# A fused attention stage: the next head's queries turned in pieces, and part of a mix moved to GpSimd

## The chip, the cores and the metric

The kernel runs on one core of one Trainium2 chip. The time is device microseconds of one execution of the whole program, here as a median over runs. The engines are named as in the profile: PE (TensorE), DVE (VectorE), ACT (ScalarE), POOL (GpSimd) and SP (SyncE).

## The reference, cut to what matters

The reference is a transformer of two blocks on 1024 rows of width 1024. The change touches only the differential attention of its first layer. That has four heads; each has two maps of 64 channels, 1024 queries, and 1280 keys (256 of the context and 1024 of the sequence), with values of 128 channels:

```python
s = jnp.einsum('bqhmd,bkhmd->bhmqk', qblk, k) * ATTN_SCALE   # m = 0, 1
p = jax.nn.softmax(s, axis=-1)
a = p[:, :, 0] - lam * p[:, :, 1]
return jnp.einsum('bhqk,bkhv->bqhv', a.astype(v.dtype), v)
```

Everything is float32. Before it stand the projections and a Fourier transform, behind it an output product, a convolution layer and a feed-forward layer; none of these is changed.

## The kernel before

**Tiles.** A head is worked in eight tiles (t = 0 to 7) of 128 queries, four heads one after the other. One loop over h = 0 to 2 ends with the passage to head h + 1 and its first two tiles; the last head is written out behind the loop. For a tile:

- PE makes the scores of map 0 and map 1, six matmuls each (`scores`, L1195), into one three-bank region of PSUM for each map.
- DVE takes the negative maximum over 1280 columns of each map (`peaks`, L1497).
- ACT exponentiates each map and sums the rows (`exps`, L859).
- DVE takes reciprocals (L1505), makes the weight of map 1 (L1507), and mixes the two maps, `mixed = prob1 * weight + prob0`, first columns 0 to 511 (`combine`), then 512 to 1279 (`combine_rest`); both are L1517.
- PE turns the mixed tile in three rounds of 4, 4 and 2 blocks (`turn`, L1211), all through the one PSUM bank MIX_BANK; DVE copies the first round out (L1532), ACT the other two (L867).
- PE multiplies by the values (`values`, L1223), and ACT finishes the tile (L876, L879).

**Order.** Each engine has its own stream, and the order in it is written out by hand; semaphores join them. In the stream of PE, `tile_step` has for tile t the scores of map 0, the second round of tile t - 2, the scores of map 1, the third round and the values of tile t - 2, and the first round of tile t - 1. In that of DVE it has for tile t the peaks of map 0, `combine` of tile t - 1, the peaks of map 1, `combine_rest` of tile t - 1, and the copy of the first round of tile t - 1.

**Passage to the next head.** Keys and queries of the next head must be turned and split into a high and a low part. POOL copies them in doubled form into `k_head` and `q_head` (L971) long ahead. At the passage PE turns the keys into the two score regions (`turn_k`, L470, ten blocks a map), ACT writes the high part (L488), DVE the low part (L497); then the same for the queries in two pieces of 1024 columns, also through the score regions (`turn_q` L470, `high_q` L493, `low_q` L504). So the first scores of the next head wait for all of it.

**POOL** has besides these copies only, in the last head, two splits of weight tiles of the next product (`out_lo`, L132, 128x1024).

## Time and profile before

| what | value |
|---|---|
| median of 3 runs | 1808.62 us (1808.35 to 1814.71) |
| span of the profiled execution, first to last instruction | 1803.4 us |
| PE, PEld busy in the span | 1742.9 us (97%), 1461.8 us (81%) |
| DVE, ACT, POOL busy | 1212.7 us (67%), 800.6 us (44%), 759.5 us (42%) |
| mean granted TensorE clock | 0.991 |

No device time is given for the profiled execution beside its span; the median of the runs stands 5.2 us above the span. The attention stage lies between about 360 and 595 us of the span. In timeline rows the first column is the start in us, the second the time until the end, then engine, line, operation, output and inputs, and in brackets the engine's idle time ahead of it and what ended it. Operations of an engine overlap a little, so the distance between two starts is shorter than the first one's duration.

### The profile page before, as it was taken

Reading aid. Unit: us, or ns where it says so; the run is one execution under the profiler, and the core shown is the slowest. Engines: PE = TensorE matmul, PEld = TensorE weight load, DVE = VectorE, ACT = ScalarE, POOL = GpSimd, SP = SyncE. Lnnn points to the kernel's source line nnn. Section 1 sums busy time; section 2 is a strip of 40 time slices with the busy share of each in tenths; the row PEclk is TensorE's granted clock in tenths of the full one; section 3 lists DMA queues with packets and bytes.
Section 4 is the critical chain, followed back from the end, with each engine's and each line's share of the span. In section 5 each row is a group of like instructions: output and inputs, shape, how many; then the busy total and the mean of one; then the engine's idle time right before and its main releaser. Section 6 shows DMA issues by size and latency. Waiting matters only on the chain.

```text
span 1803.4 us, 22828 instructions
## 1 busy us (share of the span) xinstructions
PE 1742.9 (97%) x8677; PEld 1461.8 (81%) x8677; DVE 1212.7 (67%) x1390; ACT 800.6 (44%) x1253; POOL 759.5 (42%) x450
## 2 busy tenths in 40 slices
PE   6999999989998899999999999999999999999999
PEld 4788887888888688788888889978888888878887
DVE  3734799578898616854545743786666667689865
ACT  3522222667677325533333432754435444444443
POOL 2332422000001142466666520548999999810000
PEclk8999999999999999999999999999999999999999
DMA  9567123000000731222221611303232232286433
GB/s 358 204 216 238 48 83 117 4 24 1 0 0 1 245 106 47 59 82 59 60 81 59 198 59 47 117 24 106 82 93 83 72 92 82 85 329 223 147 122 123
DMA packets 165385, 188.32 MB, mean 104 GB/s; under 512 B 9454, under 2 KB 117543, under 8 KB 165159
## 3 DMA queue, kind: packets, MB, share of 16 engines
q1 hardware_dynamic: 165287, 187.00, 31.7%
q8 instruction: 64, 1.05, 0.2%
q14 instruction: 34, 0.28, 0.1%
HBM read 152.37 MB, written 34.60 MB: 104 GB/s over the span
## 4 chain that ended last, share of the span: by engine, by line
PE 53%; DVE 4%; ACT 2%; issue 1%; DMA 1%; SPq 0%; ACTq 0%; DVEq 0%
PE ps L3217 20%; PE ps L2225 15%; PE ps L3268 10%; PE ps L2285 5%; PE ps L3568 1%; PE ps L3230 1%; DVE cv_lo_p L132 1%; DVE up_lo_p L132 1%; DVE residual L2147 0%; ACT residual L3404 0%; PE ps L3234 0%; DVE residual L3126 0%; DMA w_raw<-in_ffn_w_out 0%; ACT cv_hi_p L129 0%; ACT residual L1964 0%
## 5 line engine op out<-in xcount | busy, mean ns | idle before, releaser
L3217 PE MATMUL ps<-up_hi_p,st_hi_p 128*128 128x512 f32 x560 | 218.7, 391 | 2.9 <-ACT residual L2935 2.9
L3217 PE MATMUL ps<-up_lo_p,st_hi_p 128*128 128x512 f32 x560 | 218.5, 390 | 0.0
L3217 PE MATMUL ps<-up_hi_p,st_lo_p 128*128 128x512 f32 x560 | 218.3, 390 | 0.0
L3268 PE MATMUL ps<-down_ring 128*128 128x512 f32 x924 | 210.9, 390 | 2.8 <-DVE down_ring L132 2.6
L3268 PEld LDWEIGHTS ps<-down_ring 128*128 128x128 f32 x924 | 173.0, 188 | 40.5 <-issue 4.0
L132 POOL TENSOR_TENSOR in_lo<-in_raw,in_hi 128x512 fp32r<-128x512 f32 (+1 forms) x54 | 96.9, 1803 | 215.5 <-ACT in_hi L129 215.5
L2225 PE MATMUL ps<-cv_hi_p,cv_st_hi_p 128*128 128x512 f32 x392 | 153.2, 391 | 2.7 <-ACT residual L1943 2.7
L2225 PE MATMUL ps<-cv_hi_p,cv_st_lo_p 128*128 128x512 f32 x392 | 153.0, 390 | 0.0
L2225 PE MATMUL ps<-cv_lo_p,cv_st_hi_p 128*128 128x512 f32 x392 | 153.0, 390 | 0.0
L2067 DVE TENSOR_TENSOR residual<-ps,residual 128x512 f32<-128x512 f32 x70 | 48.3, 691 | 120.0 <-PE ps L2225 120.0
L132 POOL TENSOR_TENSOR st_lo_p<-up_raw,st_hi_p 128x512 fp32r<-128x512 f32 x68 | 101.7, 1499 | 64.4 <-ACT st_hi_p L129 64.4
L3217 PEld LDWEIGHTS ps<-up_hi_p,st_hi_p 128*128 128x128 f32 x560 | 105.5, 188 | 25.4 <-issue 3.3
L3217 PEld LDWEIGHTS ps<-up_lo_p,st_hi_p 128*128 128x128 f32 x560 | 105.6, 189 | 21.9
L3217 PEld LDWEIGHTS ps<-up_hi_p,st_lo_p 128*128 128x128 f32 x560 | 105.6, 189 | 21.9
L3068 DVE TENSOR_TENSOR residual<-ps,residual 128x512 f32<-128x512 f32 x100 | 68.4, 686 | 69.5 <-PE ps L3217 69.2
L1497 DVE TENSOR_REDUCE neg_peak<-ps 128x1 f32<-128x1280 f32 x64 | 95.2, 1487 | 9.8 <-PE ps L1195 8.6
L983 PE MATMUL ps<-in_hi,h_hi 128*128 128x512 f32 x256 | 99.8, 390 | 1.6 <-issue 0.9
L983 PE MATMUL ps<-in_hi,h_lo 128*128 128x512 f32 x256 | 99.6, 389 | 0.0
L983 PE MATMUL ps<-in_lo,h_hi 128*128 128x512 f32 x256 | 99.6, 389 | 0.0
L859 ACT ACTIVATE prob<-ps,neg_peak 128x1280 f32<-128x1280 f32 x64 | 84.9, 1326 | 29.5 <-DVE neg_peak L1497 29.2
L3087 DVE SCALAR_TENSOR_TENSOR residual<-residual,cols 128x1023 f32<-128x1023 f32 x44 | 72.5, 1648 | 35.8 <-ACT residual L2949 29.8
L132 POOL TENSOR_TENSOR cv_st_lo_p<-cv_raw,cv_st_hi_p 128x512 fp32r<-128x512 f32 x50 | 74.7, 1501 | 51.8 <-ACT cv_st_hi_p L129 51.7
(396 smaller groups left out, 4232.4 us busy)
## 6 DMA issues: line engine op xcount, KB each, us to landing
up_raw<-in_ffn_w_in SPq DMA_DIRECT2D x44, 512.0 KB, 5.0
w_raw<-in_ffn_w_out SPq DMA_DIRECT2D x66, 256.0 KB, 2.8
cv_raw<-in_odd_w_in SPq DMA_DIRECT2D x32, 512.0 KB, 5.5
in_raw<-in_even_w_in SPq DMA_DIRECT2D x48, 256.0 KB, 3.9
y_scratch<-residual SPq DMA_DIRECT2D x22, 512.0 KB, 2.6
ada_raw<-in_ada_w SPq DMA_DIRECT2D x16, 512.0 KB, 9.1
square<-in_ada_w SPq DMA_DIRECT2D x16, 512.0 KB, 4.3
rest_odd<-in_ada_w SPq DMA_DIRECT2D x16, 512.0 KB, 4.4
```

The costliest lines, as they stand in the source:

```text
L132: return eng.tensor_tensor(dst, src, high.bitcast(F32), ALU.subtract).then_inc(done, 1)
L859: act.activation(prob[:, t % 2, m, :], place(h, t, m), ACT.Exp, bias=neg_peak[:, t, m:m + 1], accum_out=total[:, t, m:m + 1]).then_inc(sem ...
L983: last = pe.matmul(ps[:, bank, :], x[:, k, r * P:(r + 1) * P], w[:, n % RING, :], start=(k == 0 and x is x_hi and w is in_hi), stop=(k == ...
L1497: dve.tensor_reduce(neg_peak[:, t, m:m + 1], place(h, t, m), AX_X, ALU.max, negate=True)\
L2067: dve.tensor_tensor(dst, ps[:, bank(g, p), :], base, ALU.add).then_inc(sem(name), 1)
L2225: last = pe.matmul(out, w[a_], x[b_], start=(first and a_ == 0 and b_ == 0), stop=(stop and a_ == 1), skip_group_check=skip)
L2285: last = pe.matmul(ps[:, 2 * (d % 4) + c, :], w[a_], x[k][:, c * BANK:(c + 1) * BANK], start=(k == 0 and a_ == 0 and x is y_hi), stop=(k = ...
L3068: dve.tensor_tensor(dst, ps[:, bank(j, p), :], base, ALU.add).then_inc(sem(name), 1)
L3087: dve.scalar_tensor_tensor(out=y[:, 1:SEQ], in0=x[:, 0:SEQ - 1], scalar=col(FFN_TAP1, first + j), in1=y[:, 1:SEQ], op0=ALU.mult, op1=ALU.a ...
L3217: last = pe.matmul(ps[:, bank(j, p), :], w[p][:, kk * P:(kk + 1) * P], x[p][:, kk, :], start=(first and w is st_hi and x is up_hi), stop=( ...
L3230: pe.matmul(ps[:, plain_bank(j, kind, side), :], part[FIRST_SLOT[j][kind, half]][:, ks], x_hi, start=(kk == 0 and half == 0 and part is st ...
L3268: last = pe.matmul(ps[:, 4 * (i % 2) + m, :], slot[:, s, m * P:(m + 1) * P], slot[:, x, :], start=(k == 0 and s == 0 and x == 2 and DOWN[i ...
```

## The change

The queries of the next head are turned in eight pieces of 256 columns (two blocks of one map), one piece in each tile, through the upper half of MIX_BANK, whose lower half the third round uses. PE turns piece p beside the third round of tile p, ACT writes its high part behind its copy of the third round, DVE its low part between `peaks(t, 1)` and `combine_rest`. The first round of the next tile, which needs the whole bank, now waits for that low part. At the passage only the keys are left, and the orders of PE, DVE and ACT there are written anew.

POOL mixes columns 1024 to 1279 of every tile in two passes (a product with the weight, then a sum), so `combine_rest` shrinks to columns 512 to 1023. POOL copies the next head's queries in the second tile of a head, once all pieces of the head before are turned, and comes to the two `out_lo` splits only behind its last mix.

```diff
+        PIECES = 8
+        def q_piece(p):
+            b = p // 2 * 2 * P
+            return q_turned[:, p % 2, b:b + 2 * P], ps[:, MIX_BANK, 2 * P:4 * P]
...
                             act.activation(mixed_t[:, t % 2, b * P:e * P],
                                            ps[:, i if is_last(h, t) else MIX_BANK, 0:(e - b) * P], ACT.Copy)\
                                .then_inc(sem(f"mix_copied{i}"), 1)
+                            if i == LAST and not isinstance(h, int):
+                                high_q(act, h + 1, t)
...
+                        def mix_end(h, t):
+                            n = h * RT + t
+                            pool.wait_ge(sem("weighed"), n + 1)
+                            pool.wait_ge(sem(f"mix_turned{LAST}"), n - 1 + CREDIT)
+                            end = mixed[:, t % 2, SEQ:KEYS]
+                            pool.tensor_tensor(end, prob[:, t % 2, 1, SEQ:KEYS], weight[:, t:t + 1].broadcast_to([P, KEYS - SEQ]), ALU.mult)\
+                                .then_inc(sem("end_weighed"), 1)
+                            pool.wait_ge(sem("end_weighed"), n + 1)
+                            pool.tensor_tensor(end, end, prob[:, t % 2, 0, SEQ:KEYS], ALU.add).then_inc(sem("mixed_end"), 1)
...
-                        def turn_q(h, m):
-                            pe.wait_ge(sem("k_low"), h * 2 + m + 1)
-                            pe.wait_ge(sem("q_twice"), h * 2 + m + 1)
-                            turn_rows(pe, score[m], q_head[:, m], RT).then_inc(sem("q_turned"), 1)
+                        def turn_q(h, p):
+                            pe.wait_ge(sem("q_twice"), h * 2 + p % 2 + 1)
+                            for i in range(2):
+                                last = pe.transpose(q_piece(p)[1][:, i * P:(i + 1) * P],
+                                                    q_head[:, p % 2, p // 2 * 2 + i, :, :].rearrange("p a d -> p (a d)"), ident[:, :])
+                            last.then_inc(sem("q_turned"), 1)
...
                             if i == 0:
                                 pe.wait_ge(sem("mixed"), n + 1 + CREDIT)
                                 pe.wait_ge(sem(f"mix_copied{LAST}"), n + CREDIT)
+                                if t == 0 or not isinstance(h, int):
+                                    pe.wait_ge(sem("q_low"), (h + 1) * PIECES + t)
...
-                            mix(t, BANK, KEYS).then_inc(sem("mixed_rest"), 1)
+                            mix(t, BANK, SEQ).then_inc(sem("mixed_rest"), 1)
...
                             peaks(h, t, 1)
+                            if t >= 2 and not isinstance(h, int):
+                                low_q(dve, h + 1, t - 2)
+                            if t == 1:
+                                low_q(dve, h, L1)
                             combine_rest(t1)
...
-                            for m in range(2):
-                                low_k(dve, h + 1, m, score[m])
-                            for m in range(2):
-                                low_q(dve, h + 1, m, score[m][:, 0:SEQ])
-                            tile_step(h + 1, 0, h, L1)
+                            low_k(dve, h + 1, 0, score[0])
+                            combine(h, L1)
+                            low_k(dve, h + 1, 1, score[1])
+                            low_q(dve, h + 1, L2)
+                            peaks(h + 1, 0, 0)
+                            combine_rest(L1)
+                            peaks(h + 1, 0, 1)
+                            turn_out(h, L1)
```

The stream of DVE in the program before, from the peaks of map 0 of one tile of the loop (negative maxima, weight, mix, copy of the first round):

```order
L1497 TENSOR_REDUCE neg_peak<-ps 128x1 [waits scored0]
L1505 RECIPROCAL inverse<-total 128x2 [waits exped1,exped0]
L1507 SCALAR_TENSOR_TENSOR weight<-total,neg_lam,inverse 128x1 [waits inverted]
L1517 SCALAR_TENSOR_TENSOR mixed<-prob,weight 128x512 [waits mix_turned2,weighed]
L1497 TENSOR_REDUCE neg_peak<-ps 128x1 [waits scored1]
L1517 SCALAR_TENSOR_TENSOR mixed<-prob,weight 128x768
L1532 COPY mixed_t<-ps 128x512 [waits o_done,mix_turned0]
```

The same tile in the changed program:

```order
L1534 TENSOR_REDUCE neg_peak<-ps 128x1 [waits scored0]
L1542 RECIPROCAL inverse<-total 128x2 [waits exped1,exped0]
L1544 SCALAR_TENSOR_TENSOR weight<-total,neg_lam,inverse 128x1 [waits inverted]
L1554 SCALAR_TENSOR_TENSOR mixed<-prob,weight 128x512 [waits mix_turned2,weighed]
L1534 TENSOR_REDUCE neg_peak<-ps 128x1 [waits scored1]
L511 REGISTER_ALU
L513 SCALAR_TENSOR_TENSOR q_turned<-ps,q_turned 64x256 [waits q_high]
L1554 SCALAR_TENSOR_TENSOR mixed<-prob,weight 128x512
L1569 COPY mixed_t<-ps 128x512 [waits o_done,mix_turned0]
```

The low part of a piece (64x256) has come in, and the second mix has 256 columns less.

The stream of PE in the changed program, in a tile of the loop from the third round on (queries L1208, third round L1248, values L1260, first round of the next tile L1248):

```order
L1208 MATMUL ps<-ident,q_head 128x128 [waits q_twice,mix_copied1,mixed_end]
L1208 MATMUL ps<-ident,q_head 128x128
L1248 MATMUL ps<-ident,mixed 128x128 x2
L1260 MATMUL ps<-residual,mixed_t 128x128 [waits o_scaled,mix_copied0]
L1260 MATMUL ps<-residual,mixed_t 128x128 x3
L1260 MATMUL ps<-residual,mixed_t 128x128 [waits mix_copied1]
L1260 MATMUL ps<-residual,mixed_t 128x128 x3
L1260 MATMUL ps<-residual,mixed_t 128x128 [waits mix_copied2]
L1260 MATMUL ps<-residual,mixed_t 128x128
L1235 REGISTER_ALU
L1238 REGISTER_ALU [waits mix_copied2,mixed]
L1248 MATMUL ps<-ident,mixed 128x128 [waits q_low]
```

Two transposes of queries have come ahead of the third round. The first round of the next tile has a wait that it did not have, for the low part of the piece (`q_low`), and it stands in front of all that PE does next.

The stream of DVE at the passage, before (low parts of keys and queries, then the first peaks of the next head):

```order
L497 TENSOR_TENSOR k_turned<-ps,k_turned 128x1280 [waits k_high]
L496 REGISTER_ALU
L497 TENSOR_TENSOR k_turned<-ps,k_turned 128x1280 [waits k_high]
L504 SCALAR_TENSOR_TENSOR q_turned<-ps,q_turned 64x1024 [waits q_high] x2
L1496 ISA
L1497 TENSOR_REDUCE neg_peak<-ps 128x1 [waits scored0]
L1505 RECIPROCAL inverse<-total 128x2 [waits exped1,exped0]
L1507 SCALAR_TENSOR_TENSOR weight<-total,neg_lam,inverse 128x1 [waits inverted]
L1517 SCALAR_TENSOR_TENSOR mixed<-prob,weight 128x512 [waits mix_turned2,weighed]
```

And in the changed program:

```order
L505 TENSOR_TENSOR k_turned<-ps,k_turned 128x1280 [waits k_high]
L1542 RECIPROCAL inverse<-total 128x2 [waits exped1,exped0]
L1544 SCALAR_TENSOR_TENSOR weight<-total,neg_lam,inverse 128x1 [waits inverted]
L1554 SCALAR_TENSOR_TENSOR mixed<-prob,weight 128x512 [waits mix_turned2,weighed]
L504 REGISTER_ALU
L505 TENSOR_TENSOR k_turned<-ps,k_turned 128x1280 [waits k_high]
L511 REGISTER_ALU
L513 SCALAR_TENSOR_TENSOR q_turned<-ps,q_turned 64x256 [waits q_high]
L1534 TENSOR_REDUCE neg_peak<-ps 128x1 [waits scored0]
L1554 SCALAR_TENSOR_TENSOR mixed<-prob,weight 128x512
L1534 TENSOR_REDUCE neg_peak<-ps 128x1 [waits scored1]
```

The mix of the last tile has moved between the two low parts of the keys, and of the queries only one piece is left there.

## Rows read from the trace of the kernel before

**Rows 1.** Timeline of DVE, one tile of head 1.

```profile
450.28 0.68 DVE L1532 COPY mixed_t<-ps 128x512 f32<-128x512 f32 x1
451.08 1.49 DVE L1497 TENSOR_REDUCE neg_peak<-ps 128x1 f32<-128x1280 f32 x1
...
452.68 0.22 DVE L1507 SCALAR_TENSOR_TENSOR weight<-total,neg_lam,inverse 128x1 f32<-128x1 f32 x1
452.93 0.75 DVE L1517 SCALAR_TENSOR_TENSOR mixed<-prob,weight 128x512 f32<-128x512 f32 x1
453.60 1.48 DVE L1497 TENSOR_REDUCE neg_peak<-ps 128x1 f32<-128x1280 f32 x1
455.00 1.01 DVE L1517 SCALAR_TENSOR_TENSOR mixed<-prob,weight 128x768 f32<-128x768 f32 x1
...
456.99 1.49 DVE L1497 TENSOR_REDUCE neg_peak<-ps 128x1 f32<-128x1280 f32 x1 [0.38 <-PE ps L1195]
```

**Rows 2.** Timeline of PE beside it: scores L1195, second round L1211.

```profile
449.63 1.40 PE L1195 MATMUL ps<-k_turned,q_turned 128*128 128x512 f32 x6
451.11 0.63 PE L1211 MATMUL ps<-ident,mixed 128*128 128x128 f32 x4
451.49 1.41 PE L1195 MATMUL ps<-k_turned,q_turned 128*128 128x512 f32 x6
...
455.54 1.41 PE L1195 MATMUL ps<-k_turned,q_turned 128*128 128x512 f32 x6
```

**Rows 3.** Timeline, head 1 from its third tile, and the passage to head 2.

```profile
433.87 1.49 DVE L1497 TENSOR_REDUCE neg_peak<-ps 128x1 f32<-128x1280 f32 x1 [0.47 <-PE ps L1195]
...
462.64 1.49 DVE L1497 TENSOR_REDUCE neg_peak<-ps 128x1 f32<-128x1280 f32 x1
...
467.18 2.35 PE L470 MATMUL ps<-ident,k_head 128*128 128x128 f32 x20
...
468.48 2.37 ACT L488 ACTIVATE k_turned<-ps 128x1280 fp32r<-128x1280 f32 x2 [0.38 <-PE ps L470]
...
469.74 2.89 DVE L497 TENSOR_TENSOR k_turned<-ps,k_turned 128x1280 fp32r<-128x1280 f32 x2 [1.57 <-ACT k_turned L488]
...
473.48 1.23 DVE L504 SCALAR_TENSOR_TENSOR q_turned<-ps,q_turned 64x1024 fp32r<-64x1024 f32 x1 [0.84 <-ACT q_turned L493]
...
476.53 1.49 DVE L1497 TENSOR_REDUCE neg_peak<-ps 128x1 f32<-128x1280 f32 x1
...
488.22 1.49 DVE L1497 TENSOR_REDUCE neg_peak<-ps 128x1 f32<-128x1280 f32 x1 [0.47 <-PE ps L1195]
```

**Rows 4.** Timeline of the last head: POOL's two splits and DVE beside them.

```profile
561.20 2.36 POOL L132 TENSOR_TENSOR out_lo<-out_raw,out_hi 128x1024 fp32r<-128x1024 f32 x1 [85.22 <-ACT out_hi L129]
561.35 2.23 DVE L1507 SCALAR_TENSOR_TENSOR weight<-total,neg_lam,inverse 128x1 f32<-128x1 f32 x1
...
568.80 0.22 DVE L1507 SCALAR_TENSOR_TENSOR weight<-total,neg_lam,inverse 128x1 f32<-128x1 f32 x1
568.85 2.40 POOL L132 TENSOR_TENSOR out_lo<-out_raw,out_hi 128x1024 fp32r<-128x1024 f32 x1 [5.29 <-ACT out_hi L129]
569.05 2.74 DVE L1517 SCALAR_TENSOR_TENSOR mixed<-prob,weight 128x512 f32<-128x512 f32 x1
```

**Rows 5.** Groups of POOL by line and shape (busy us, mean ns, idle).

```profile
L2560 POOL TENSOR_TENSOR odd_sums<-up_raw,odd_sums 128x512 f32<-128x512 f32 x10 | 12.9, 1294 | 0.8
L971 POOL COPY k_head<-residual 128x1280 f32 x6 | 7.4, 1254 | 146.4 <-PE ps L470 89.3 <-PE ps L1112 57.1
```

**Rows 6.** Timeline of DVE and POOL at two later places.

```profile
1150.65 1.49 DVE L250 TENSOR_TENSOR residual<-residual,cv_staged 128x512 f32<-128x512 f32 x2
1152.22 1.26 POOL L2555 TENSOR_TENSOR odd_sums<-up_raw 128x512 f32<-128x512 f32 x1 [7.01 <-DVE residual L250]
...
1478.54 2.42 DVE L3087 SCALAR_TENSOR_TENSOR residual<-residual,cols 128x1023 f32<-128x1023 f32 x1
1478.59 1.29 POOL L2555 TENSOR_TENSOR residual<-up_raw 128x512 f32<-128x512 f32 x1
```

More of the change, by code:

```diff
@@ L488, in high_k, with high_q @@
             act.activation(k_turned[:, m, 0, :], src, ACT.Copy).then_inc(sem(k + "_high"), 1)
-        def high_q(act, h, m, src, q="q"):
-            act.wait_ge(sem(q + "_turned"), h * 2 + m + 1)
-            act.activation(q_turned[:, m, :], src, ACT.Copy, scale=ATTN_SCALE).then_inc(sem(q + "_high"), 1)
+        PIECES = 8
+        def q_piece(p):
+            b = p // 2 * 2 * P
+            return q_turned[:, p % 2, b:b + 2 * P], ps[:, MIX_BANK, 2 * P:4 * P]
+        def high_q(act, h, p):
+            dst, src = q_piece(p)
+            act.wait_ge(sem("q_turned"), h * PIECES + p + 1)
+            act.activation(dst, src, ACT.Copy, scale=ATTN_SCALE).then_inc(sem("q_high"), 1)
         def low_k(dve, h, m, src, k="k"):
@@ L521, in program @@
         CREDIT = 2
-        credited = ["mixed", "mixed_rest", f"mix_turned{LAST}", f"mix_copied{LAST}", "o_done", "o_scaled"]
-        credited += [x + state for x in "kq" for state in ("_twice", "_turned", "_high", "_low")]
+        credited = ["mixed_end", "mixed", "mixed_rest", f"mix_turned{LAST}", f"mix_copied{LAST}", "o_done", "o_scaled"]
+        credited += ["k" + state for state in ("_twice", "_turned", "_high", "_low")] + ["q_twice"]
+        credited_pieces = ["q_turned", "q_high", "q_low"]
         L1, L2 = RT - 1, RT - 2
@@ L965, in _ @@
                         pool.wait_ge(sem("y_f_done"), F_GROUPS)
-                        with pool.Fori(1, HEADS) as h:
-                            for name, dst, src in (("k", k_head, k_nat), ("q", q_head, q_nat)):
-                                pool.wait_ge(sem(name + "_turned"), h * 2)
+                        def mix_end(h, t):
[7 more added lines that the diff above has]
+                            pool.tensor_tensor(end, end, prob[:, t % 2, 0, SEQ:KEYS], ALU.add).then_inc(sem("mixed_end"), 1)
+                        with pool.Fori(0, HEADS - 1) as h:
+                            for name, dst, src, pieces in (("k", k_head, k_nat, 2), ("q", q_head, q_nat, PIECES)):
+                                if name == "q":
+                                    mix_end(h, 0)
+                                pool.wait_ge(sem(name + "_turned"), (h + 1) * pieces)
                                 for m in range(2):
-                                    pool.tensor_copy(dst[:, m, :, :, :], head_columns(src, h, m))\
+                                    pool.tensor_copy(dst[:, m, :, :, :], head_columns(src, h + 1, m))\
                                         .then_inc(sem(name + "_twice"), 1)
+                            for t in range(1, RT):
+                                mix_end(h, t)
+                        for t in range(RT):
+                            mix_end(HEADS - 1, t)
                         for m in range(OUT_FIRST):
@@ L1208, in turn @@
                                     pe.wait_ge(sem("mixed_rest"), n + 1 + CREDIT)
+                                if i == LAST:
+                                    pe.wait_ge(sem("mixed_end"), n + 1 + CREDIT)
                                 pe.wait_ge(sem(f"mix_copied{i - 1}"), n + 1)
+                            if i == LAST and not isinstance(h, int):
+                                turn_q(h + 1, t)
                             for j in range(b, e):
@@ L1263, in _ @@
                             turn(h, L2, 1)
-                            turn_q(h + 1, 0)
+                            values(h, L2, 0)
                             turn(h, L2, 2)
-                            turn_q(h + 1, 1)
-                            for m in range(2):
-                                scores(h + 1, 0, m)
-                            for i in range(3):
-                                values(h, L2, i)
+                            values(h, L2, 1)
+                            scores(h + 1, 0, 0)
+                            values(h, L2, 2)
+                            scores(h + 1, 0, 1)
                             turn(h, L1, 0)
@@ L1548, in _ @@
                             dve.sem_inc(sem(name), CREDIT)
+                        for name in credited_pieces:
+                            dve.sem_inc(sem(name), PIECES)
                         dve.tensor_scalar(subln_gain[:, :], col(SUBLN, 0), 1.0 - LAMBDA_INIT, None, ALU.mult)
@@ L1569, in _ @@
                             tiles(h)
-                            for m in range(2):
-                                low_k(dve, h + 1, m, score[m])
-                            for m in range(2):
-                                low_q(dve, h + 1, m, score[m][:, 0:SEQ])
-                            tile_step(h + 1, 0, h, L1)
+                            low_k(dve, h + 1, 0, score[0])
[6 more added lines that the diff above has]
+                            turn_out(h, L1)
                             tile_step(h + 1, 1, h + 1, 0)
```

22 lines of the change are left out of this document (13 added, 9 removed).

## The prediction, on record before the run

> **What bounds the kernel now.** The page first: PE is busy for 97% of the span and DVE for 67%, but that mixes stages, so I read the attention stage by itself. Its timelines of PE and DVE, side by side for one tile, say what each tile waits for. From the peaks of map 0 in tile 2 to those in tile 7 takes 28.77 us, 5.75 a tile [rows 3]. The tile shown takes 5.91, and at its end DVE stands 0.38 us idle until PE has the scores [rows 1]; so three of the five take 5.65. PE begins scores at 449.63 and again at 455.54, also 5.91 us, and in between its second round starts only at 451.11 [rows 2], just behind the end of DVE's copy of the first round at 450.96 [rows 1]: a wait of some 0.26 us, the amount by which the long tile is longer, so PE's own work is 5.65. DVE's own is close: 2.52 us from peaks 0 to peaks 1, 1.40 to the second mix, 1.01 less an overlap of 0.08 for it, 0.68 for the copy, in all 5.53 [rows 1]. Two engines are thus nearly level, and what counts is who waits for whom.
>
> The second thing to see is the passage between heads: from the peaks of tile 7 (462.64) to the first peaks of the next head (476.53) takes 13.89 us instead of 5.75, and to the third tile (488.22) 25.58 us [rows 3]. The third is the last head: when POOL runs a split that reads SBUF, a DVE instruction with two inputs in SBUF stands still. A weight of one column takes 2.23 us instead of 0.22, and a mix 2.74 instead of 0.75; both end about when POOL's instruction does, the mix after another 0.54 us [rows 1, 4].
>
> **The change part by part.**
>
> *Tiles of the first three heads.* DVE loses 256 columns of the mix: 1.01 against 0.75 us, 0.26 less [rows 1]. It gains the low part of a piece. Before, 64x1024 takes 1.23 us [rows 3]; at the mix's slope (0.26 us per 256 columns) a quarter is 1.23 - 3 x 0.26, or 0.43 us, 0.35 of it until the next start. Bounds: 0.31 (a quarter of 1.23) and 0.51 (0.20 more than that). Alone these would leave DVE at 5.6 us and PE, with two transposes more (ten take half of 2.35 less overlap, 0.11 each [rows 3]), at 5.65 + 0.2 = 5.87. But the new wait ties both into a ring. PE may not make the first round of the next tile before the low part is done; behind that stand the scores of map 0, and DVE needs those for its peaks. Round the ring: peaks 0 to peaks 1 2.52, peaks 1 to its successor 1.40, low part 0.43, to PE 0.05 (scores end 451.03, peaks start 451.08), first round to scores 0.38, scores 1.41, back to DVE 0.05 [rows 1 to 3]. That is 6.24 us, say 6.23, against 5.75. The second mix and the copy run beside PE and no longer count, so the 0.26 us saved buys nothing here. From tile 2 to tile 7 before: 462.64 - 433.87 = 28.77 [rows 3]; after: 5 x 6.23 = 31.15. Three heads: **+7.1**. With the piece at its bounds, +5.3 to +8.3.
>
> *The passage.* Before, 25.58 us from tile 7 to tile 2. After, from the peaks of tile 7 as zero: low part of piece 5 done at 4.35, PE's first round until 4.78, ten key blocks until 6.03, ACT's high part until 7.32, DVE's low_k(0) from 7.37, 1.40 to the combine, which takes 1.12, low_k(1) 1.40, low part of piece 6 0.35: next peaks at 11.64, against 13.89. The durations are halves of the 2.35, 2.37 and 2.89 us rows [rows 3]. Then peaks 1.40, second mix, peaks 1.40, copy 0.68: 0.67 for the mix, but POOL's copies of keys (two of 1.25 [rows 5]) now lie beside it. If they hold up a two-input instruction as the splits do, 0.6 more, and the peaks of tile 1 come at 16.4. Next ACT's exponentials of tile 0, PE's scores of tile 1, piece 7, third round, values, first round, scores: 1.41 + 1.30 + 0.18 + 0.21 + 2.24 + 0.35 + 1.41 behind the peaks that end at 15.8, with the steps between engines, about 23.0. Gain 2.5 us at each of two passages. At the third, POOL has no keys left to copy, so 3.1. Together **-8.1**; if POOL's copies hold nothing up, -9.3; if the steps that I took from halves cost 0.5 more each time, -6.6.
>
> *The last head.* It has no pieces, so no ring. The two splits no longer fall among its tiles: their two delays were 2.01 and 1.99 us, less about 0.35 each that DVE had to spare: -3.3. PE's 5.65 us a tile then rules, with ACT's split of a weight tile still costing one tile some of it back: -0.3. At the end all three rounds of the last tile wait for POOL's second pass, 0.8 us later than DVE's own mix would be, and the splits come just then, beside two-input multiplications of DVE: 0.4 more. **-2.4** in all, between -4.0 and 0 (the second split, 2.40 us [rows 4], blocking its full length).
>
> *POOL's mix elsewhere.* 512 columns take 1.29 us, 1024 take 2.36 [rows 4, 5], so 256 take about 0.75 a pass. Bounds: 0.65, half of 1.29, and 1.29, if a short one is no faster. DVE's mix starts 0.03 us behind the weight (452.90 to 452.93 [rows 1]). POOL starts 0.08 us behind what releases it (1152.14 to 1152.22 [rows 6]). So DVE comes first by 0.05, POOL's first pass waits for it, and ends 1.4 us behind the weight, its second at 2.25, while DVE reads PSUM for the peaks. PE needs the result a tile later: the cost is nothing. That cover is gone where POOL comes first, which is the first rival.
>
> The sum: 7.1 - 8.1 - 2.4 = -3.4 us. Against the profiled span of 1803.4 that gives 1800.0; the median of the runs is 5.2 above the span, hence **1805.2 us** against 1808.6.
>
> **The rivals.**
>
> *GpSimd takes the shared way first (slower).* The margin of 0.05 us is small. At 1478.54 a DVE instruction with two inputs in SBUF is recorded as starting 0.05 before POOL's, and still stands until POOL is done: 2.42 us, 1.29 for POOL and 1.08 for itself [rows 6]. For it: the same 0.05. Against it: that one overlapped its predecessor, while at 568.80 an instruction released by a wait, as the mix is, got through in 0.22 us with POOL 0.05 behind [rows 4]. If POOL wins, the mix ends at 0.08 + 0.75 + 0.54 = 1.37 us behind the weight instead of 0.78: 0.6 us more in each tile, in the ring too. On 15 intervals in loop tiles 9.0, at the passages 2.2, in the last head and at the start 2.2: +13.4, hence **1818.6 us**. It decides from the point where POOL's lock is taken before DVE's.
>
> The Trainium skill, "SBUF — State Buffer", section "Who interferes with whom", says that whichever of the two issues first gets the shared pair for the whole instruction. By that rule DVE's lead of 0.05 would settle it for my forecast; by the row at 1478.54 it need not, for there the first to be recorded lost. I keep the rival.
>
> *The new wait is covered (faster).* If PE reached the first round later than the low part, the ring would be open and PE's 5.87 us would rule: 0.36 less on the 15 intervals and a little at the passages, 5.4 + 1, hence **1799 us**. Against it: PE ends the values about 0.35 us ahead of the low part by the sum above. For it only a piece at its lower bound.
>
> *POOL is slow.* At 1.29 us a pass both passes last past 3.4 us behind the weight and stand in front of DVE's second mix in the last head and at the passages: 6 us more, **1811 us**. It is the copy at 1.25 us for 1280 columns that speaks against a fixed price.
>
> *The change does nothing measurable.* It would show as 1808.6 with tiles still at 5.75; the waits in the stream speak against that, though the sum can come to the same time.
>
> **How the numbers follow.** Forecast 0.60, with a range of its own from 1801.5 to 1810 out of the bounds (pieces -1.8 and +1.2, passage -1.2 and +1.5, last head -1.6 and +2.4, not all at once). GpSimd first 0.22. Wait covered 0.09. POOL slow 0.09. About 0.5%, 9 us, is what a measurement can tell from no change: faster means under 1799.6, slower over 1817.7. Half of the covered case and a little of the forecast's tail is faster, 0.06. Of the GpSimd case two thirds lie beyond 1817.7, and 0.04 comes from both troubles at once: 0.19. The rest, 0.75, is the same. The range 1800 to 1819.5 takes in the forecast, slow POOL and most of the GpSimd case.
>
> **What would show it.** Right: peaks 0 to peaks 0 at 6.2 us in heads 0 to 2 and 5.65 in the last, PE idle about 0.35 us before the first round, released by the low part; 11.6 us from tile 7 to the next head; DVE's first mix still 0.75; no weight or mix over 1 us in the last head's tiles; POOL's first pass about 1.3 us, its second 0.75. Wrong: a first mix of about 1.3 us (GpSimd first), tiles at 5.9 (wait covered), both POOL passes over 1.2 (slow).

## The result, and the profile of the changed kernel

The changed kernel takes **1822.57 us** (median of 4 runs, 1822.23 to 1827.24); the kernel before, on the same chip, 1811.33 (4 runs, 1808.35 to 1814.71). The ratio is 1.0072 [1.0054, 1.0090]: slower by 0.7%, where I forecast 1805.2 and a range up to 1819.5. The span is 1820.8 us and the mean granted clock 0.986, where the kernel before had 0.991.

Two numbers separate what the change did from what the rest of the program did by itself. From the first peaks of head 0 to the first gate multiplication behind the heads (I call it the stage from here on) the kernel before takes 231.35 us in its profile and the changed one 242.96: **11.6 us more**. Behind the gate, where the code is the same, it was 1208.4 us before and 1213.8 now, and over all profiles of this study, in no order that the edits explain, 1208.2 to 1213.9; so 5.4 of the 17.4 us between the two spans belong to no edit. I compare kernels by their stage, and give the time beside it.

DVE's timeline, one tile of head 1 in the changed kernel (columns as before), and POOL's beside it:

```profile
440.24 1.21 DVE L1554 SCALAR_TENSOR_TENSOR mixed<-prob,weight 128x512 f32<-128x512 f32 x1
441.37 1.48 DVE L1534 TENSOR_REDUCE neg_peak<-ps 128x1 f32<-128x1280 f32 x1
442.88 0.43 DVE L513 SCALAR_TENSOR_TENSOR q_turned<-ps,q_turned 64x256 fp32r<-64x256 f32 x1
443.34 0.75 DVE L1554 SCALAR_TENSOR_TENSOR mixed<-prob,weight 128x512 f32<-128x512 f32 x1
444.12 0.69 DVE L1569 COPY mixed_t<-ps 128x512 f32<-128x512 f32 x1
445.22 1.49 DVE L1534 TENSOR_REDUCE neg_peak<-ps 128x1 f32<-128x1280 f32 x1 [0.41 <-PE ps L1226]
```

```profile
440.29 0.61 POOL L983 TENSOR_TENSOR mixed<-prob,weight 128x256 f32<-128x256 f32 x1 [3.32 <-DVE weight L1544]
440.98 1.06 POOL L986 TENSOR_TENSOR mixed<-mixed,prob 128x256 f32<-128x256 f32 x1
```

Against [rows 1], DVE's first mix takes 1.21 us where the same 512 columns took 0.75. POOL's first pass is recorded 0.05 us behind it and takes 0.61, undisturbed: POOL went first, and DVE stood until it was done. The mix without a POOL pass beside it (443.34) takes 0.75 as ever. POOL's second pass is the one that waits now, for the rest of DVE's mix (1.06 instead of the 0.73 that it takes undisturbed). The groups show the same for all 32 tiles:

```profile
L986 POOL TENSOR_TENSOR mixed<-mixed,prob 128x256 f32<-128x256 f32 x32 | 33.8, 1056 | 2.5
L983 POOL TENSOR_TENSOR mixed<-prob,weight 128x256 f32<-128x256 f32 x32 | 19.6, 613 | 153.7 <-DVE weight L1544 153.7
L1554 DVE SCALAR_TENSOR_TENSOR mixed<-prob,weight 128x512 f32<-128x512 f32 x64 | 64.1, 1004 | 1.9
```

PE's timeline in the same tile, where [rows 2] has the second round as the one that waits:

```profile
443.36 0.66 PE L1248 MATMUL ps<-ident,mixed 128*128 128x128 f32 x4 [0.60 <-DVE q_turned L513]
443.77 1.41 PE L1226 MATMUL ps<-k_turned,q_turned 128*128 128x512 f32 x6
```

The ring that I had forecast is there: low part of the piece (442.88), PE's first round (443.36, idle for 0.60 us before it), scores (443.77), peaks (445.22). Everything that DVE does late between the peaks of map 0 and the low part therefore goes into the tile in full, and the 0.46 us of the first mix stand in exactly that place. A tile takes 6.83 us in heads 0 to 2, at every tile. The list of waits has the two lines that were not there before (us in total, times, longest):

```profile
PEld ps L1248 <- DVE q_turned L513: 17.0, 21, 0.9
PE ps L1248 <- DVE q_turned L513: 12.7, 19, 0.7
```

The stage in pieces, from the starts of the peaks of map 0 in DVE's timeline (before: [rows 3]):

| | before | change | forecast |
|---|---|---|---|
| tiles 2 to 7, heads 0, 1, 2 | 29.10, 28.77, 28.75 | 34.13 each: +15.8 | +7.1 |
| tile 7 to tile 2 of the next head | 25.33, 25.58, 25.58 | 24.47, 24.49, 24.25: -3.3 | -8.1 |
| last head, tiles 2 to 7, then to the gate | 32.10, 20.40 | 29.87, 21.78: -0.9 | -2.4 |
| the stage | 231.35 | 242.96: +11.6 | -3.4 |

### The profile page after: what moved, and what is told of

The parts are those of the page before. It is cut to its first block, busy times and chain, and to the rows that moved or that the text cites. A ratio compares the mean times of both kernels' runs of the same rounds, so it can differ in the third digit from the quotient of the medians.

```text
span 1820.8 us, 23099 instructions
## 1 busy us (share of the span) xinstructions
PE 1752.3 (96%) x8677; PEld 1470.2 (81%) x8677; DVE 1224.0 (67%) x1408; ACT 801.2 (44%) x1271; POOL 813.3 (45%) x514
## 4 chain that ended last, share of the span: by engine, by line
PE 54%; DVE 4%; ACT 2%; issue 1%; DMA 0%; SPq 0%; ACTq 0%; DVEq 0%
PE ps L3263 20%; PE ps L2271 14%; PE ps L3314 11%; PE ps L2331 5%; PE ps L3614 1%; PE ps L3276 1%; DVE cv_lo_p L132 1%; DVE up_lo_p L132 1%; DVE residual L2193 0%; ACT residual L3450 0%; PE ps L3280 0%; DVE residual L3172 0%; DMA w_raw<-in_ffn_w_out 0%; ACT cv_hi_p L129 0%; ACT residual L2010 0%
## 5 line engine op out<-in xcount | busy, mean ns | idle before, releaser
L1226 PE MATMUL ps<-k_turned,q_turned 128*128 128x512 f32 (+1 forms) x384 | 91.3, 373 | 6.1 <-ACT prob L870 5.7
```

The costliest lines, as they stand in the source:

```text
L1226: last = pe.matmul(place(h, t, m)[:, b:e], q_turned[:, m, t * P:(t + 1) * P], k_turned[:, m, part, b:e], start=(part == 0), stop=(part == 1))
```

## The experiments

My theory: the change is made of two parts that each cost a little, and the rest of the 11.6 us comes from POOL going first where the ring (low part, first round, scores, peaks) passes the delay on. The rivals: the pieces alone make the loss (a longer ring than I reckoned); POOL's work costs wherever it lies; the lost columns and not the order make the mix slow. The result of all eleven runs first; each is told below. "five tiles" is tile 2 to tile 7 in head 1, "passage" the one behind head 1.

| run | stage | five tiles | passage | last head | time, ratio to before |
|---|---|---|---|---|---|
| before | 231.35 | 28.77 | 25.58 | 32.10 + 20.40 | |
| change | 242.96 | 34.13 | 24.49 | 29.87 + 21.78 | 1822.57, 1.0072 |
| e1 pieces alone | 234.73 | 31.83 | 23.86 | 32.08 + 20.39 | 1815.39, 1.0018 [1.0001, 1.0035] |
| e2 POOL's mix alone | 235.57 | 29.51 | 26.29 | 29.76 + 22.77 | 1815.27, 1.0025 [1.0012, 1.0038] |
| e3 POOL behind the mix | 232.95 | 31.86 | 23.27 | 28.87 + 22.56 | 1810.67, 0.9998 [0.9983, 1.0014] |
| e4 ring opened, POOL behind | 231.41 | 30.70 | 23.50 | 28.88 + 23.82 | 1810.98, 1.0000 [0.9985, 1.0014] |
| f1 wide pass and a wait | 233.63 | 31.86 | 23.48 | 29.76 + 21.79 | 1812.35, 1.0007 [0.9990, 1.0024] |
| f2 POOL's mix alone, behind | 228.44 | 28.45 | 25.04 | 28.87 + 22.54 | 1806.83, 0.9977 [0.9958, 0.9996] |
| f3 splits moved, alone | 228.45 | 28.77 | 25.57 | 29.07 + 20.41 | 1807.70, 0.9982 [0.9964, 0.9999] |
| f4 both of these | 225.82 | 28.46 | 25.05 | 28.89 + 20.41 | 1805.48, 0.9967 [0.9947, 0.9987] |
| g1 one wait more | 233.44 | 31.87 | 23.10 | 29.76 + 22.76 | 1813.84, 1.0013 [0.9995, 1.0031] |
| g2 wide pass, no wait | 255.02 | 36.25 | 25.81 | 29.77 + 24.00 | 1832.88, 1.0118 [1.0066, 1.0169] |
| f5 e4 with f4's last head | 229.32 | 30.75 | 23.50 | 28.88 + 21.55 | 1806.37, 0.9975 [0.9957, 0.9992] |

**The clock in these stages.** Two places of the stage carry the granted TensorE clock, and it differs between profiles of the same instructions. From 16 to 8 us ahead of the gate it is 1.00 (2.4 GHz) in the kernel before, the change, e1, f1, f3 and f4, 0.79 in e2, e3, f2, g1 and f5, and 0.57 in e4 and g2. In the change and in g1, where PE has the same instructions, PE stands idle for the same 1.38 us ahead of its last ten transposes. In g1 the clock is then 0.50 (1.2 GHz) from 584 to 587 us, and in the change it stays at 1.00. The forty matmuls with the values behind that, in the change and in g1:

```profile
595.43 4.63 PE L1260 MATMUL ps<-residual,mixed_t 128*128 128x128 f32 x40
...
584.37 6.02 PE L1261 MATMUL ps<-residual,mixed_t 128*128 128x128 f32 x40
```

The way to the gate is 21.78 and 22.76 us there, so about 1.0 us is the clock's. g2 at 0.57 takes 24.00, 2.2 more. The other place is head 0: from 8 to 24 us behind the first peaks the clock is 0.89 in the kernel before, the change, e1, f3, f4 and g1, and 0.79 in the rest. f2 and f4, the same code up to the last head, take 29.31 and 28.88 us for head 0's five tiles, and 28.45 and 28.46 for head 1's. By these rows the stages of e2, e3, f2 and f5 hold about 1.5 us of the clock that the change and the kernel before do not, e4 and g2 about 2.7, g1 1.0 and f1 0.5; these are estimates. Why it falls in one profile and not in another is open.

**Each part alone (e1, e2).** e1 is the change without `mix_end` and its waits, DVE mixing all 1280 columns; e2 is the kernel before with `mix_end` added and nothing of the pieces.

```diff
# e1, against the changed kernel
-                            for t in range(1, RT):
-                                mix_end(h, t)
...
-                            mix(t, BANK, SEQ).then_inc(sem("mixed_rest"), 1)
+                            mix(t, BANK, KEYS).then_inc(sem("mixed_rest"), 1)
```

> The queries in pieces as in the change, but DVE mixes columns 512 to 1279 again and POOL mixes nothing. Theory A (POOL's first pass takes the shared way from DVE's first mix, 0.46 us in every tile, and all of it lands in the ring): first mix back to 0.75 us, tiles of heads 0 to 2 at 6.35 to 6.4 us instead of 6.84, the two delays of 2 us by the splits back in the last head, total 5 to 8 us under the changed kernel. Theory B (the new wait and PE's two more transposes make the loss, POOL's passes are hidden): tiles stay at 6.8 and the total within 2 us of the changed kernel, or above it by the 256 columns more.

> The kernel before, with POOL mixing the last 256 columns behind the weight, queries turned as before. Theory A: first mix 1.21 us as in the changed kernel, but no ring, so part of the 0.46 us is paid by the 256 columns less: tiles at 5.7 to 5.9 us against 5.75, passages 1 us longer, no delays by the splits in the last head; total 0 to 3 us above the kernel before. Theory B: tiles at 5.65, total 3 us below the kernel before.

The pieces alone make the stage 3.4 us longer, POOL's mix alone 4.2, together 7.6 of the 11.6. In e1 the first mix is back at 0.75 and a tile takes 6.37: the ring without POOL. In e2 there is no such ring; a tile averages 5.9 instead of 5.75, so that 0.46 us of a slow first mix is mostly taken up by DVE's slack and PE's. The remaining 4.0 us are the two meeting: in the ring there is no slack, and the 0.46 counts whole (6.83 - 6.37). The fifteen tiles of the change are 6.6 us above those of e1, near 15 times 0.46. In e1 all times came as expected; e2 came out worse, by 4.6 us in the medians where I had 0 to 3, and by 4.2 in the stage, some 1.5 of them the clock's.

**The order changed (e3).** In `mix_end` POOL waits until DVE's first mix is done:

```diff
-                            pool.wait_ge(sem("weighed"), n + 1)
+                            pool.wait_ge(sem("mixed"), n + 1 + CREDIT)
```

> The changed kernel, but POOL's first pass waits for DVE's first mix instead of for the weight, so DVE is always first. Theory A: first mix 0.75 us, POOL's passes 0.6 and 0.65 us side by side with the peaks, tiles of heads 0 to 2 at 6.35 us (ring alone), last head 5.65; total 8 to 10 us under the changed kernel, within 2 us of the kernel before. Theory B: no change of more than 2 us. Theory C (the lock is held for longer than POOL's instruction, or the second mix is hit instead): second mix at 1.2 us, gain under 4 us.

The stage falls by 10.0 us to 232.95, the tiles to 6.37. POOL's passes (0.61 and 0.73) now start 0.83 to 0.92 us behind DVE's first mix, beside the peaks, which read PSUM, and in these tiles they hold up nothing. That is most of the loss, and it leaves the kernel level with the one before. The tiles of e1 and e3 are equal, 6.37, though DVE's second mix takes 1.02 us in e1 and 0.75 in e3: as forecast, time saved there buys nothing in the ring.

**One wait more (f1, g1).** f1 was to double POOL's first pass, so as to see what DVE's stall grows with. It needed a buffer, and I put a wait in front of the pass for it, in heads 0 to 2 only, on a semaphore that has long reached its value.

> The change, but in the tiles of heads 0 to 2 GpSimd's first pass goes over the last 512 columns (into a buffer beside; its second pass takes the 256 that it needs from there; the output is the same). This measures what DVE's first mix loses when both run at once: in the change 1.21 us instead of 0.75, beside a GpSimd pass of 0.61. Theory A (GpSimd holds the way to SBUF for its whole instruction, and DVE does its work behind it): the pass takes about 1.15 to 1.2 us, and DVE's first mix grows by the same 0.55 or so, to 1.75 us; the tiles go from 6.83 to about 7.4 us, five of them from 34.1 to 36.9, and the stage grows by some 10 us or more. Theory B (a fixed price of a collision, or both slowed by a share): the mix stays at 1.21, or grows by less than half of what the pass does, and the tiles stay under 7.1 us.

The experiment as I meant it failed, and showed more than it was made for. The two timelines, heads 1 and 3 of the same run, DVE's mix and POOL's pass:

```profile
444.29 0.75 DVE L1560 SCALAR_TENSOR_TENSOR mixed<-prob,weight 128x512 f32<-128x512 f32 x1
444.41 1.53 POOL L989 TENSOR_TENSOR spare_end<-prob,weight 128x512 f32<-128x512 f32 x1 [4.04 <-DVE weight L1550]
...
548.49 1.20 DVE L1560 SCALAR_TENSOR_TENSOR mixed<-prob,weight 128x512 f32<-128x512 f32 x1
548.53 0.61 POOL L989 TENSOR_TENSOR mixed<-prob,weight 128x256 f32<-128x256 f32 x1 [5.08 <-DVE weight L1550]
```

With the wait, POOL is recorded 0.12 us behind DVE, and DVE goes first: its mix takes 0.75 us although the pass beside it is twice as wide. Without the wait, in head 3, POOL is 0.04 behind and goes first. g1 takes the width away and keeps the wait, now in all heads:

```diff
+                            pool.wait_ge(sem("mixed_end"), n + CREDIT)
                             end = mixed[:, t % 2, SEQ:KEYS]
```

> The change with one more wait in front of GpSimd's first pass, on a semaphore that has long reached its value (its own second pass of the tile before), and nothing else. In the run with the wide pass this wait stood in front in heads 0 to 2 only: there GpSimd was recorded 0.12 us behind DVE's first mix and DVE kept its 0.75 us, while in its last head, without the wait, GpSimd was 0.04 to 0.05 behind and DVE took 1.20. Theory A (only the order of arrival within some 0.1 us decides who goes first): with the wait, GpSimd is recorded 0.12 behind, DVE's first mix is 0.75 us in all four heads, GpSimd's first pass is recorded as 1.2 to 1.3 us because it waits for DVE's, the tiles are 6.37 us and the stretch from first peaks to the gate 233 us, 10 less than the change's 243; time 1811 to 1812.5 where the change has 1822.6. Theory B (it was the width of the pass, or the buffer beside, that let DVE through): first mix 1.2 us, tiles 6.83, the stretch 243.

DVE's first mix and then POOL's first pass, in heads 1 and 3 of g1:

```profile
442.20 0.75 DVE L1555 SCALAR_TENSOR_TENSOR mixed<-prob,weight 128x512 f32<-128x512 f32 x1
...
551.69 1.20 DVE L1555 SCALAR_TENSOR_TENSOR mixed<-prob,weight 128x512 f32<-128x512 f32 x1
```

```profile
442.33 1.10 POOL L984 TENSOR_TENSOR mixed<-prob,weight 128x256 f32<-128x256 f32 x1 [4.47 <-DVE weight L1545]
...
551.74 0.61 POOL L984 TENSOR_TENSOR mixed<-prob,weight 128x256 f32<-128x256 f32 x1 [3.90 <-DVE weight L1545]
```

One wait that waits for nothing takes 9.5 us off the stage (242.96 to 233.44), 10.5 without g1's fall of the clock: POOL stands 0.12 to 0.14 us behind DVE in heads 0 to 2, the mix takes 0.75 and the tiles 6.37. In the last head, where the expectation was the same, it did not come true: there POOL is again 0.05 behind and first, although the wait stands in front. That head is written out, and its waits compare with constants, while in the loops they compare with a register; the delay of about 0.08 us seems to come with the latter. I tried nothing to separate that.

**What the stall grows with (g2).** The wide pass without the wait: two buffers instead of one make it needless.

```diff
-                            pool.tensor_tensor(end, prob[:, t % 2, 1, SEQ:KEYS], weight[:, t:t + 1].broadcast_to([P, KEYS - SEQ]), ALU.mult)\
...
+                                spare = spare_end[:, t % 2, :]
+                                b, first, product = KEYS - BANK, spare, spare[:, BANK - (KEYS - SEQ):BANK]
+                            pool.tensor_tensor(first, prob[:, t % 2, 1, b:KEYS], weight[:, t:t + 1].broadcast_to([P, KEYS - b]), ALU.mult)\
```

> The change with GpSimd's first pass over 512 columns in heads 0 to 2 (into a buffer of two halves beside, so that no further wait is needed; the output is the same). GpSimd should now be recorded 0.04 to 0.05 us behind DVE as in the change, and go first. Its pass of 512 columns takes 0.90 us by itself, as the wide pass in the earlier run took after DVE had ended, or up to 1.2. Theory A (DVE stands for GpSimd's whole instruction): DVE's first mix grows from 1.21 us by what the pass grows, 0.4 to 0.6, to 1.65 to 1.8 us, and tiles from 6.83 to 7.3 to 7.4. Theory B (a fixed price, or a shared rate): the mix stays within 0.2 us of 1.21, tiles under 7.05.

The same two instructions in head 1 of g2:

```profile
445.73 1.64 DVE L1560 SCALAR_TENSOR_TENSOR mixed<-prob,weight 128x512 f32<-128x512 f32 x1
```

```profile
445.78 1.04 POOL L989 TENSOR_TENSOR spare_end<-prob,weight 128x512 f32<-128x512 f32 x1 [3.32 <-DVE weight L1550]
```

POOL's pass grew by 0.43 us (0.61 to 1.04), DVE's mix by 0.43 to 0.44 (1.21 to 1.64), the tile by 0.42 (6.83 to 7.25). DVE stands for the whole of POOL's instruction and then does its own work; in both cases it ends 0.55 us behind POOL. A fixed price is out. f1 and g2 have the same pass over 512 columns and differ in 0.08 us of POOL's start: 21 us of stage, about 2 of them the clock's. g2 was executed only twice (1829.13 and 1836.64 us); its tiles repeat to 0.03 us.

**The ring opened (e4).** e3, and ScalarE copies the upper half of each piece to SBUF as well, from where DVE takes the low part; PE's first round then waits for ScalarE's copy alone.

```diff
-                                    pe.wait_ge(sem("q_low"), (h + 1) * PIECES + t)
+                                    pe.wait_ge(sem("q_high"), (h + 1) * PIECES + t)
```

> As the run before this one, and ACT also copies the upper half of each piece (64x256) to SBUF, from where DVE makes the low part; the first round of the next tile waits for ACT's copy and no more for DVE. If the ring through the low part is what holds tiles at 6.35 us, it is open now: tiles of heads 0 to 2 at 5.85 to 6.0 us, PE's own work, no PE idle time ahead of the first round; total 14 to 16 us under the changed kernel and 4 to 7 us under the kernel before. If instead DVE's added work is what counts, tiles stay above 6.2 us and it is equal to the run with POOL behind.

The tiles fall from 6.37 to 6.05 and 6.27 by turns, not to 5.9. PE no longer waits for the low part, but DVE's own tile is 0.3 us longer than before (from its rows 2.52 + 1.51 + 0.46 + 0.67 + 0.68, or 5.84 instead of 5.53), and in the longer tiles its copy of the first round comes late for PE's second. And a second ring stands behind the first, through ScalarE:

```profile
450.61 0.38 ACT L504 ACTIVATE q_raw<-ps 64x256 f32<-64x256 f32 x1
451.02 1.33 ACT L872 ACTIVATE prob<-ps,neg_peak 128x1280 f32<-128x1280 f32 x1
452.24 0.19 ACT L872 ACTIVATION_READ_ACCUMULATOR prob<-ps,neg_peak 128x1 f32 x1
452.49 1.45 PE L1228 MATMUL ps<-k_turned,q_turned 128*128 128x512 f32 x6
```

The next tile's scores of map 0 wait for ScalarE's exponentials of map 0, which end at 452.43, 0.06 us ahead of them, and ScalarE comes to these only behind the copy that this edit added. In e3 the same exponentials end 0.9 us ahead of such scores (442.17 and 443.09). That ScalarE holds the tiles is read from these rows and not tested by a run. The stage is 231.41: what is saved between heads against the kernel before (1.9 to 2.6 us each time, 6.5 in all) is lost in the tiles (6.4 us). I had expected 4 to 7 us less time than the kernel before; the two are level (1810.98 and 1810.64).

**POOL's mix alone, in the right place (f2); the splits alone (f3); both (f4).** f2 is e2 with e3's line. f4 is f2 and f3 together, and DVE mixes all of the very last tile itself. f3 is the kernel before with POOL's splits of the output weights placed where DVE reads PSUM:

```diff
-                        for m in range(OUT_FIRST):
+                        for t, m, b, e in ((4, 0, 0, 4), (5, 0, 4, 8), (7, 1, 0, 8)):
                             pool.wait_ge(sem("out_high"), m + 1)
-                            split_low(pool, out_first[m][1][:, :, :], out_raw[m][:, :, :], out_first[m][0][:, :, :], sem("out_low"))
+                            pool.wait_ge(sem("mixed_rest"), (HEADS - 1) * RT + t + 1 + CREDIT)
+                            split_low(pool, out_first[m][1][:, b:e, :], out_raw[m][:, b:e, :], out_first[m][0][:, b:e, :], sem("out_low"))
```

> The kernel before with GpSimd's mix of the last 256 columns, begun only behind DVE's first mix, and without the pieces (queries are turned between heads as before). Theory A (GpSimd's mix as such is nearly free, what cost 4.2 us in the run with GpSimd's mix alone was its start beside DVE's first mix): DVE's first mix 0.75 us, tiles of heads 0 to 2 at PE's own 5.65 us (five of them 28.3 where before has 28.8 to 29.1 and that run 29.5 to 30.0), passages 25.6 to 26 us, last head's five tiles 28.5 to 29 instead of 32.1, behind them 22 to 22.5 instead of 20.4 because PE's last three rounds wait for GpSimd's end and the two splits come then. The stretch from the first peaks to the gate 229.6 us, 1.7 less than before; time 1808 to 1809.5 where before has 1810. Theory B (GpSimd's passes slow DVE or delay PE wherever they lie): tiles stay at 5.8 or more, the stretch at 233 or more.

> The kernel before with nothing but GpSimd's two splits of output weights moved in the last head: the first in two halves, each begun behind DVE's second mix of tiles 4 and 5, the second behind that of tile 7, so that they lie beside copies and peaks that read PSUM. This measures my term for the last head by itself. Theory A (the two splits cost that head their two stalls of 2.0 us less DVE's slack): its five tiles 28.6 us instead of 32.1, no weight or mix over 1 us, 20.4 us behind them as before, the stretch from first peaks to the gate 227.8, 3.5 less; time about 1806.5 where before has 1810. Theory B (PE was late there anyway, by ScalarE's own splits of these weights): five tiles at 30.5 or more, the stretch 1.5 us less at most.

> Both of the last two together, and DVE mixes all of the very last tile itself, so that nothing at the end of the stage waits for GpSimd. Theory A: tiles of heads 0 to 2 at 28.3 for five, last head 28.6 and 20.4 behind it, the stretch 227.3 us, 4 less than before; time 1806. Theory B (GpSimd's mix and the splits take each other's gain, since DVE has no slack left in the last head once PE's 5.65 us rules): no less than the run with the moved splits alone, 227.8 or more.

All three came out as the first theory said. f2 and f4 are 1.2 and 1.5 us better than expected, mostly in the passages (25.0, where I had 25.6 to 26); f3 is 0.65 us worse, 0.47 of it in the tiles of its last head (29.07 for 28.6). f2 takes 2.9 us off the stage although its profile has both falls of the clock, f3 2.9 and f4 5.5 without them. The same POOL instructions as in e2 (235.57) cost 7.1 us less when they start some 0.8 us later (228.44), with the same clock in both. f4 beats both kernels: 1805.48 against 1810.44 for the kernel before beside it, ratio 0.9967 [0.9947, 0.9987]. Its last head, DVE and POOL around the first half of a split, where [rows 4] has 2.23 and 2.74:

```profile
566.84 0.22 DVE L1528 SCALAR_TENSOR_TENSOR weight<-total,neg_lam,inverse 128x1 f32<-128x1 f32 x1
567.10 0.75 DVE L1538 SCALAR_TENSOR_TENSOR mixed<-prob,weight 128x512 f32<-128x512 f32 x1
```

```profile
563.77 1.29 POOL L132 TENSOR_TENSOR out_lo<-out_raw,out_hi 128x512 fp32r<-128x512 f32 x1 [0.71 <-DVE mixed L1538]
567.93 0.61 POOL L973 TENSOR_TENSOR mixed<-prob,weight 128x256 f32<-128x256 f32 x1 [2.86 <-DVE mixed L1538]
568.62 0.73 POOL L976 TENSOR_TENSOR mixed<-mixed,prob 128x256 f32<-128x256 f32 x1
```

**The pieces at their best (f5).** e4 with the last head of f4.

> The best that I can make of the pieces: GpSimd behind DVE's first mix, DVE's low part read from a copy in SBUF that ScalarE makes (so that PE's first round needs no low part), the two splits moved as in the run with the splits moved, and DVE mixing all of the very last tile. It differs from the version without pieces that took 1805.5 us (stretch 225.8) in the pieces alone. Theory A (the pieces add to each tile 0.4 to 0.6 us, on PE and on DVE, and give back about 1.7 us at each passage): five tiles 30.7 instead of 28.5 us, passages 23.3 instead of 25.0, last head 28.9 and 20.4, the stretch 227.5 to 228, about 2 more than without pieces; time 1807.5. Theory B (the pieces pay once nothing else is in the way): the stretch under 225.8, time under 1805.5.

Stage 229.32, 3.5 us more than f4, which differs in the pieces alone; I had expected 2. Tiles and passages of head 1 came as expected. The way to the gate, where the code is f4's, took 21.55 us and not 20.4, at a granted clock of 0.79 where f4 has 1.00 (from 16 to 8 us ahead of the gate). Head 0's five tiles took 31.74, 2.9 more than in f4, where heads 1 and 2 have 2.3 more; there the clock fell too. Without these two, 1.1 and 0.6 us, the pieces cost 1.8, as expected. The times (1806.37 and 1805.48) do not tell the two apart; the stages do. The pieces do not pay even when nothing else is in their way.

## Why the prediction was wrong

**The step that failed** is "So DVE comes first by 0.05, POOL's first pass waits for it ... the cost is nothing". The recorded starts were as I wrote, DVE 0.04 to 0.05 us ahead, and POOL went first all the same, in every tile: DVE's mix took 1.20 to 1.21 us, and the cost that I had put at nothing was 0.46 us in each tile of the ring. With the order turned (e3, g1) the mix takes 0.75 and the stage 10.0 and 9.5 us less. I had the counterexample in hand, the instruction at 1478.54 that lost with the same 0.05 [rows 6], and set against it the weight at 568.80, which got through [rows 4]. That one is a single column, a poor stand-in for a mix of 512; the row at 1478.54 was the nearer one. I gave that rival 0.22 and priced it at 1818.6. Its price was right in kind: it said 0.6 us a tile, and 0.46 was measured, because POOL's pass took 0.61 us and not the 0.75 that I had reckoned. It said the ring would pass it on, and it did. In stage: change less g1 is 9.5 us, 6.8 in the tiles and 3.6 in the passages, less 0.9 in the last head, where g1 still has POOL first and loses 1.0 by the clock; the rival had 9.0 in the tiles, 2.2 in the passages and 2.2 in the last head and at the start, 13.4 in all.

The Trainium skill, "SBUF — State Buffer", section "Who interferes with whom", says of VectorE's 2-port modes that whoever issues first gets the shared pair, the SBUF ports that the two engines have in common, for the whole instruction. It says besides that a VectorE instruction with two inputs in SBUF contends with a GpSimd instruction that reads SBUF. On the length the trace agrees, for two inputs too: the stall grew by 0.43 when the pass did. On who is first, the start in the profile does not say who issued first: 0.04 to 0.05 us ahead DVE lost, 0.12 to 0.13 ahead it won.

**The other terms**, read from g1 for heads 0 to 2, since it has DVE first there as I assumed. Its stage is +2.1 against before, 1.0 of it the clock's, where my sum had -3.4:

- *Tiles, +7.1 forecast, +9.0 measured* (3 x 31.87 against 86.62). The ring closed as described, at 6.37 us instead of 6.23. Two terms were short. From the peaks of map 1 to the low part I took 1.40, the step to an instruction that overlaps its predecessor. The low part starts behind the peaks' end, 1.51 us (441.37 to 442.88 in the change), and so does the mix behind the low part (443.34). The trace before had shown this already: its second low part at a passage starts at 475.27 and takes 1.23 us, and the peaks behind it start at 476.53 [rows 3], with no overlap. And from PE's first round to the scores it is 0.41 instead of 0.38. The piece itself took the forecast 0.43.
- *Passages, -8.1 forecast, -6.9 measured in g1 and -3.3 in the change.* To the first peaks of the next head it is 12.08 us in g1 and 12.98 in the change, forecast 11.64. The change's 0.90 more is the stall of the first mix, twice. Of the 0.44 between forecast and g1, 0.33 is the same missing overlap, three times: the two low parts of pieces start 0.11 us later than in my sum, and the peaks behind the second another 0.11. From there to the third tile the change takes 11.51 and g1 11.02, forecast 11.36. Of the 1.2 us that g1 misses, 0.9 is the third passage: there I took off 0.6 for POOL having no keys left to copy, and it takes 23.37 us where the others take 23.12 and 23.10. One mix of the last head, which is slow again, lies in it (0.45); in the change, where all are slow, the third is 0.24 shorter than the second. So POOL's copies cost a passage about 0.2 us, not 0.6.
- *Last head, -2.4 forecast, -0.9 measured in the change (0.0 in g1, where POOL is first there too, and where the way to the gate took another 1.0 us at a granted clock of 0.79 instead of 1.00).* f3 prices the moved splits by themselves: -3.0, my -3.6 (3.3 and 0.3) less 0.6. The five tiles lose 0.8 of it to POOL going first (29.87 against 29.07), and the way to the gate 1.4 (21.78 against 20.41), where I had 1.2: 0.8 for POOL's second pass and 0.4 for the splits.
- *From span to time, 5.2 us.* Every run that has both shows its time 1.75 to 1.99 us above its span, 1.8 on average. By that the profiled execution before took about 1805.2 us (an estimate), one of the faster ones, and I compared its span with a median of others. That made my number 3.4 us higher than its own sum and has nothing to do with the change.

Right were the ring, its place and the row that shows it (PE idle before its first round, released by the low part), the cost of the piece, the freed last head, and that POOL is not slow: 0.61 us a pass, under my 0.65 to 1.29.

## What to carry to other kernels

Work that is given to GpSimd beside VectorE costs by where it starts before it costs by how much it is: released by the same event as a VectorE instruction with two inputs in SBUF, it may go first and stop VectorE for its whole length, and a lead of 0.05 us in the profile did not save it here. Release it from the end of that instruction, so that it lies beside work on PSUM (here 7 to 10 us for one changed wait). And before adding a wait into a loop of two engines that are nearly level, add up the ring that it closes: inside it, every delay counts in full, and in its tiles time saved outside it counts nothing. Look at the granted clock of each stretch before a difference of 1 us between two profiles is given to an edit.

## What the hardware showed that I had not expected

- A wait on a semaphore that has long reached its value moved POOL's start by 0.07 to 0.10 us in the heads of the loop, and with it the order of two engines and 9.5 us of the stage. The same wait in the last head left the start at 0.04 to 0.05 us. That a register or a constant in the wait makes the difference is not shown.
- POOL's copy of the queries, with one input in SBUF, also holds up a mix of DVE with two: in the changed kernel it covers DVE's second mix in the step of tile 1 of heads 1 and 2, which takes 1.20 and 1.19 us instead of 0.75.

```profile
436.31 1.20 DVE L1554 SCALAR_TENSOR_TENSOR mixed<-prob,weight 128x512 f32<-128x512 f32 x1
```

```profile
434.95 2.02 POOL L994 COPY q_head<-fq 128x1024 f32 x2
```

- POOL's two passes over 256 columns are not alike: 0.61 us for the product with a weight of one column, 0.73 for the sum of two buffers, each undisturbed.
